# Recurrence of a two-part network: inverse blocks across the array's halves, step products on four quarters, narrower masked copies, both half products ahead of the steps

## The reference, cut to what matters

```python
def rwkv7_scan(r, w, k, v, kk, a):
    def step(state, inp):
        r_t, w_t, k_t, v_t, kk_t, a_t = inp
        sa = jnp.einsum('bhvk,bhk->bhv', state, -kk_t)
        state = (state * w_t[:, :, None, :] + sa[..., None] * (kk_t * a_t)[:, :, None, :]
                 + v_t[..., None] * k_t[:, :, None, :])
        return state, jnp.einsum('bhvk,bhk->bhv', state, r_t)
    ...
    _, out = lax.scan(step, jnp.zeros((nB, H, N, N), F32), xs)
```

## Time and profile before

| | |
|---|---|
| runs | 2591.47, 2591.73, 2594.94 us; median 2591.73 |
| profiled execution | span 2590.2 us; no time outside the span is listed for it |
| PE busy | 2488.4 us, 96% |
| DVE busy | 1104.5 us, 43% |
| ACT busy | 475.8 us, 18% |
| POOL busy | 179.1 us, 7% |
| the 80 copies at L3948 | the first at 2068.1, the last at 2337.4 us |
| a middle pair, from one first half product to the next | 35.4 us |

### The profile page before, as it was taken

The page is one execution under the profiler, slowest core; times in us unless marked ns, Lnnn a source line. Parts: engine busy times, 40 slices in busy tenths (PEclk is TensorE's granted clock), DMA queues, the critical chain, the costliest instruction groups (busy, mean ns, idle before and its releaser), DMA issues. The chain is left out here.

```text
span 2590.2 us, 80261 instructions
## 1 busy us (share of the span) xinstructions
PE 2488.4 (96%) x36137; PEld 2147.1 (83%) x36137; DVE 1104.5 (43%) x2659; ACT 475.8 (18%) x1059; POOL 179.1 (7%) x225
## 2 busy tenths in 40 slices
PE   8999999999999999999999999899999999999998
PEld 7898878789889989999989898677768677877775
DVE  4672554468211010110110102457672578775676
ACT  2112000211123223210000001410010444542000
POOL 0100000010022322210000000000000001110000
PEclk9999999999989999999999999999999999999999
DMA  7444444554589999999999998335653000020443
GB/s 228 156 147 149 162 162 149 162 163 147 208 317 407 407 407 408 407 408 407 407 407 408 407 407 277 122 98 194 220 172 130 3 7 7 7 70 25 163 172 120
DMA packets 289906, 571.50 MB, mean 221 GB/s; under 512 B 17422, under 2 KB 180244, under 8 KB 289764
## 3 DMA queue, kind: packets, MB, share of 16 engines
q1 hardware_dynamic: 289764, 569.49, 60.0%
HBM read 568.37 MB, written 5.28 MB: 221 GB/s over the span
## 5 line engine op out<-in xcount | busy, mean ns | idle before, releaser
L2669 PE MATMUL ps<-xg,ring 128*64 128x80 f32 x14336 | 508.4, 233 | 6.4 <-issue 4.8
L2669 PEld LDWEIGHTS ps<-xg,ring 128*64 128x64 f32 x14336 | 501.8, 137 | 11.0 <-issue 6.6
L2792 DVE TENSOR_TENSOR hidden<-acted,ps 128x320 f32<-128x320 f32 x64 | 28.6, 446 | 662.2 <-PE ps L2669 662.2
L2685 PE MATMUL ps<-hidden,expert_down 128*64 128x80 f32 x7168 | 258.4, 234 | 11.0 <-DMA expert_down<-in_moe_w_down_dram 5.2
L2685 PEld LDWEIGHTS ps<-hidden,expert_down 128*64 128x64 f32 x7168 | 252.8, 138 | 13.9 <-issue 9.7
L2734 ACT ACTIVATE ring<-second 128x1792 f32<-128x1792 f32 x60 | 101.9, 1699 | 212.7 <-PE ps L2669 156.3
L631 PE MATMUL ps<-xT,ring 128*128 128x256 f32 (+1 forms) x592 | 134.4, 387 | 3.0 <-PEq L474 3.0
L631 PEld LDWEIGHTS ps<-xT,ring 128*128 128x128 f32 (+1 forms) x592 | 108.0, 185 | 26.7 <-issue 3.5
L2726 POOL COPY ring<-second 128x1792 f32<-128x1792 f32 x60 | 101.0, 1683 | 311.1 <-PE ps L2669 183.8
L631 PE MATMUL ps<-ring,xT 128*128 128x256 f32 (+1 forms) x544 | 108.9, 361 | 2.2 <-PEq L1136 2.2
L631 PEld LDWEIGHTS ps<-ring,xT 128*128 128x128 f32 x544 | 96.0, 190 | 14.5 <-issue 3.0
(11 more groups left out here) (617 smaller groups left out, 3980.4 us busy)
## 6 DMA issues: line engine op xcount, KB each, us to landing
expert_down<-in_moe_w_down_dram SPq DMA_DIRECT2D x96, 1024.0 KB, 17.1
ring<-in_mlp_w_dram SPq DMA_DIRECT2D x64, 1024.0 KB, 5.3
ring<-in_moe_w_gate_dram SPq DMA_DIRECT2D x68, 896.0 KB, 16.0
ring<-in_moe_w_up_dram SPq DMA_DIRECT2D x68, 896.0 KB, 16.6
second<-in_moe_w_gate_dram SPq DMA_DIRECT2D x30, 1792.0 KB, 18.8
second<-in_moe_w_up_dram SPq DMA_DIRECT2D x30, 1792.0 KB, 19.0
ring<-in_w_xkv_dram SPq DMA_DIRECT2D x16, 1024.0 KB, 5.4
expert_down<-in_moe_w_down_dram SPq DMA_DIRECT2D x32, 512.0 KB, 16.5
```

What stands on the lines that cost most here:

```text
L2669: mm = pe.matmul(bank[b][o:o + HEAD, at, :], w[:, c, f * P + o:f * P + o + HEAD], xg[:, p * E_STEP + c, :], start=(p == 0 and c == 0 and a ...
L2685: mm = pe.matmul(yT[c // 4][o:o + HEAD, c % 4, :], w[:, j, c * P + o:c * P + o + HEAD], hidden[:, f, :], start=False, stop=False, skip_gro ...
L2792: dve.tensor_tensor(hidden[:, part, :], acted[:, part, :], src, ALU.mult).then_inc(hidden_ready, 1)
```

## The change

- The mask `level` is cut to 64 columns: for each level the columns of the upper kind that can change, then those of the lower kind. `XX` and `M1` are flat arrays of 9 x 64 now, in two regions of 4 x 64 (kind 0 and kind 1, swapped for d = 1). `moved` picks, out of both regions, the half of the columns that a level can change: runs of 2^k columns, with as many left out between them. The copies in `front` and `step` move these alone: 256 elements per partition in place of 512, at the last level 128 in place of 256.
- The transposed kind lies on the other half of the partitions. `halves` takes its operands from half h and writes to the other half; `steps` has one kind's results on half b and the other kind's on the other half, and one kind in bank A(d), the other in bank B(d) (`made`). So its products go over all four quarters in turn.
- `m1` writes what `XX` now expects; `right_sides`, `take_right`, `solve_first`, `carry`, `take_carried` and `solve_second` change halves accordingly, and the first solve's result goes to bank B(1) (`FIRST`).
- In each level `halves` of both directions come first, at level 1 each with its `rows`; then for each direction the level's other products and `steps`. In the last pair `turn(6)` comes behind the carries.
- The order of DVE, ACT, POOL and SP stays.

```diff
-        level.append(np.tile(np.concatenate([lower, lower.T, lower], axis=1), (2, 1)))
+        low_columns = lower[:, (e[0] // b) % 2 == 0]
+        high_columns = lower.T[:, (e[0] // b) % 2 == 1]
+        level.append(np.tile(np.concatenate([low_columns, high_columns], axis=1), (2, 1)))
...
-        M1 = [tmp(ctx, "M1", [P, 4, 2, HEAD]) for _ in range(2)]
-        XXs = [[tmp(ctx, "XX", [P, 4, 2, HEAD]) for _ in range(2)] for _ in range(2)]
+        M1 = [tmp(ctx, "M1", [P, 9 * HEAD]) for _ in range(2)]
+        XXs = [[tmp(ctx, "XX", [P, 9 * HEAD]) for _ in range(2)] for _ in range(2)]
...
+        def region(kind, d):
+            return kind if d == 0 else 1 - kind
+
+        def XX(i, d, kind, n):
+            at = (4 * region(kind, d) + n) * HEAD
+            return XXs[d][i % 2][:, at:at + HEAD]
+
+        def whole(i, d):
+            return XXs[d][i % 2][:, 0:8 * HEAD]
+
+        def moved(flat, k):
+
+            b = 1 << k
+            regions = flat[:, 0:2 * (4 * HEAD + b)].rearrange("p (r x) -> p r x", r=2)[:, :, 0:4 * HEAD]
+            return regions.rearrange("p r (n m z b) -> p r n m z b", n=4, z=2, b=b)[:, :, :, :, 0, :]
+
+        def places_of(k):
+            b = 1 << k
+            return level[:, k, :].rearrange("p (r m b) -> p r m b", r=2, b=b).unsqueeze(2).to_broadcast([P, 2, 4, HEAD // 2 // b, b])
...
+        FIRST = B(1)
+
+        def both_kinds(d):
+
+            return ps[:, A(d):B(d) + 1, :].rearrange("p a b -> p (a b)")[:, 4 * HEAD:]
+
+        def made(d, kind, n):
+
+            at = n * HEAD
+            if region(kind, d):
+                return ps[:, B(d), at:at + HEAD]
+            return ps[:, A(d), 4 * HEAD + at:4 * HEAD + at + HEAD]
...
                 def halves(i, k, d):
                     wait(pe, "x_ready", i, 2 * (k - 1) + d + 1)
                     for n in range(4):
                         for b in range(2):
-                            h = half(b)
-                            mm = pe.matmul(ps[h, A(d), n * HEAD:(n + 1) * HEAD], GM[d][h, n, 0, h], XX(i, d)[h, n, 0, :], start=True, stop=True)
+                            h, other = half(b), half(1 - b)
+                            mm = pe.matmul(ps[other, A(d), n * HEAD:(n + 1) * HEAD], GM[d][h, n, 0, h], XX(i, d, 0, n)[h], start=True, stop=True)
                     mm.then_inc(q["half_done"].sem, 1)
...
-                                h = half(b)
-                                xt, p = XX(i, d)[h, n, 1, :], Pb[d][h, n, :]
-                                at = (2 * n + kind) * HEAD
-                                mm = pe.matmul(ps[h, B(d), at:at + HEAD], p if kind else xt, xt if kind else p, start=True, stop=True)
+                                other = half(1 - b)
+                                xt, p = XX(i, d, 1, n)[other], Pb[d][other, n, :]
+                                on = other if kind else half(b)
+                                mm = pe.matmul(made(d, kind, n)[on], p if kind else xt, xt if kind else p, start=True, stop=True)
...
                             halves(i, k, d)
                             if k == 1:
                                 rows(i, d)
+                        for d in range(2):
+                            if k == 1:
                                 rest(i, 0, d)
...
                     outputs(i, 0, 1)
+                    for d in range(2):
+                        carry(i, 1, d)
                     if last:
                         turn(6)
-                    for d in range(2):
-                        carry(i, 1, d)
...
-                    places = level[:, 0, d * HEAD:(d + 2) * HEAD].unsqueeze(1).to_broadcast([P, 4, 2 * HEAD])
-                    dve.copy_predicated(XX(j, d)[:].rearrange("p n k e -> p n (k e)"), places, M1[d][:].rearrange("p n k e -> p n (k e)"))
+                    dve.copy_predicated(moved(XXs[d][j % 2][:], 0), places_of(0), moved(M1[d][:], 0))
...
-                    x = XX(i, d)[:].rearrange("p n k e -> p n (k e)")
-                    made = ps[:, B(d), :].rearrange("p (n e) -> p n e", n=4)
-                    a, e = (HEAD if k == LEVELS - 1 else 0), 2 * HEAD
-                    places = level[:, k, d * HEAD + a:d * HEAD + e].unsqueeze(1).to_broadcast([P, 4, e - a])
-                    dve.copy_predicated(x[:, :, a:e], places, made[:, :, a:e]).then_inc(q["x_ready"].sem, 1)
+                    x, fresh, places = moved(XXs[d][i % 2][:], k), moved(both_kinds(d), k), places_of(k)
+                    if k == LEVELS - 1:
+                        x, fresh, places = (z[:, region(1, d)] for z in (x, fresh, places))
+                    dve.copy_predicated(x, places, fresh).then_inc(q["x_ready"].sem, 1)
```

More of the change, by code:

```diff
@@ L3078, in __init__ @@
         self.keep = tmp(ctx, "keep", [P, 2, 3 * P])
-        self.level = tmp(ctx, "level", [P, LEVELS, 3 * HEAD], I32)
+        self.level = tmp(ctx, "level", [P, LEVELS, HEAD], I32)
         self.eyes = tmp(ctx, "eyes", [P, HEAD])
@@ L3449, in begin @@
                     for d in range(2):
-                        act.activation(XX(j, d)[:].rearrange("p n k e -> p (n k) e"), eyes[:].unsqueeze(1).to_broadcast([P, 8, HEAD]), ACT.Copy).then_inc(q["x_begun"].sem, 1)
+                        act.activation(whole(j, d).rearrange("p (n e) -> p n e", e=HEAD), eyes[:].unsqueeze(1).to_broadcast([P, 8, HEAD]), ACT.Copy).then_inc(q["x_begun"].sem, 1)
                 def exps_first(j, d):
@@ L3581, in m1 @@
                         for kind in range(2):
-                            for hh, b in CORNERS:
+                            at = (2 * region(kind, d) + t) * HEAD
+                            for hh, on in CORNERS:
+                                b = 1 - on if kind else on
                                 a, e = KR(j, d)[half(hh), t, 0, half(b)], Bs[d][half(hh), t, half(b)]
-                                at = (2 * t + kind) * HEAD
-                                mm = pe.matmul(ps[half(b), A(d) + hh, at:at + HEAD], e if kind else a, a if kind else e, start=True, stop=True)
+                                mm = pe.matmul(ps[half(on), A(d) + hh, at:at + HEAD], e if kind else a, a if kind else e, start=True, stop=True)
                     mm.then_inc(q["m1_done"].sem, 1)
@@ L3642, in right_sides @@
                         left = GM[d][:, 2 * t + hh, 2, :]
[L3643 to L3644 removed]
+                        pe.matmul(ps[g, G(d), at:at + HEAD], left[:, f], values(i, t, hh), start=(hh == 0), stop=(s == 0 and hh == 1))
+                        mm = pe.matmul(ps[f, G(d), at:at + HEAD], left[:, g], values(i, t, hh), start=(hh == 0), stop=False)
                     if s:
                         s0 = S0[d][:].rearrange("p a b -> p (a b)")
[L3647 to L3648 removed]
+                        pe.matmul(ps[g, G(d), RIGHT:RIGHT + P], KR(i, d)[:, t, 0, f], s0, start=False, stop=True)
+                        mm = pe.matmul(ps[f, G(d), RIGHT:RIGHT + P], KR(i, d)[:, t, 0, g], s0, start=False, stop=False)
                     mm.then_inc(q["right_done"].sem, 1)
@@ L3675, in solve_first @@
                     wait(pe, "right_ready", i, 2 * s + d + 1)
-                    f = half(d)
+                    f, g = half(d), half(1 - d)
                     for hh in range(2):
                         at = SOLVED + hh * HEAD
-                        mm = pe.matmul(ps[f, G(d), at:at + HEAD], XX(i, d)[f, 2 * chunk(s, d) + hh, 1, :], rhs[d][f, s, hh, :], start=True, stop=True)
+                        mm = pe.matmul(ps[f, FIRST, at:at + HEAD], XX(i, d, 1, 2 * chunk(s, d) + hh)[g], rhs[d][g, s, hh, :], start=True, stop=True)
                     mm.then_inc(q["first_done"].sem, 1)
@@ L3686, in carry @@
                         at = RIGHT + hh * HEAD
-                        mm = pe.matmul(ps[g, G(d), at:at + HEAD], GM[d][f, 2 * t + hh, 0, g], sa[d][f, t, hh, :], start=False, stop=(hh == 1))
+                        mm = pe.matmul(ps[f, G(d), at:at + HEAD], GM[d][f, 2 * t + hh, 0, g], sa[d][f, t, hh, :], start=False, stop=(hh == 1))
                     mm.then_inc(q["carried_done"].sem, 1)
@@ L3691, in solve_second @@
                     wait(pe, "carried_ready", i, 2 * s + d + 1)
-                    g = half(1 - d)
+                    f, g = half(d), half(1 - d)
                     for hh in range(2):
                         at = SOLVED + hh * HEAD
-                        mm = pe.matmul(ps[g, G(d), at:at + HEAD], XX(i, d)[g, 2 * chunk(s, d) + hh, 1, :], rhs[d][g, s, hh, :], start=True, stop=True)
+                        mm = pe.matmul(ps[g, G(d), at:at + HEAD], XX(i, d, 1, 2 * chunk(s, d) + hh)[f], rhs[d][f, s, hh, :], start=True, stop=True)
                     mm.then_inc(q["second_done"].sem, 1)
```

10 lines of the change are left out of this document (4 added, 6 removed).

## The result

The changed kernel takes **2603.57 us** (median of six runs, 2597.07 to 2612.8), the kernel before 2592.15 on the same chips (six runs, 2591.47 to 2594.94). The ratio is 1.0046, 95% interval 1.0029 to 1.0063: **slower by about half a per cent**, and more scattered. The forecast was 2589.7 and "no change"; the time lies inside the range of 2575 to 2605, the sign was given 0.26.

What follows compares the result with a forecast made beforehand. It took the bound to be the chain between PE's products and DVE's in-order queue, not either engine's busy time. Six middle pairs +1.2, first -0.5, last -2.7: -2.0 us, 2588.2 profiled, 2589.7 median; range 2575 to 2605.

Steps and rivals of the forecast that it cites:

- no change: The worked forecast for the whole kernel: within 0.2% (5.2 us) of the kernel before; chance 0.43 in all.
- the sign: Whole kernel slower than before: chance 0.26, against 0.31 for faster and 0.43 for within 0.2%.
- S in four quarters: Step's product at levels 1 to 4 goes from 0.93 to 0.47 us: 29.8 us less work for PE.
- Rival C: In the step's product, row halves sharing a bank take turns, so it stays 0.93: slower, 2605 us; chance 0.06.
- The order eats the gain: Direction 1's half product, put forward, waits for DVE's copy; middle pair 0.2 us longer despite 3.7 less PE work.
- Rival B: DVE's pieces don't hold up direction 1's half products; the full 29.8 us come out: 2562, half 2577; chance 0.20.
- The short copies: Masked copies of 256 elements last 0.44 us and hold DVE's queue 0.34, in place of 0.72 and 0.62.
- its other case: Front copies: if single words cost what the length saved, level 1, direction 1's half product comes 0.23 us later; 1.8 total.
- Rival D: Masked copies keep 0.62 us of queue because runs are short: 2.3 per pair, about 17 in all, 2607; chance 0.08.
- The last pair: Recurrence's last pair, without factor pieces on DVE: last result at 20.98, 2.7 us shorter than before.
- The first pair: Recurrence's first pair, without output pieces on DVE: result at 23.14, 0.5 us shorter than before.
- rival E: PE's idle spots in each pair halve the clock for a tenth of the recurrence: 10 to 15 us, 2603; chance 0.06.

Runs made afterwards that it cites:

- order_hold: Kernel before with both half products first in each level, plus 2, 1 and 2 unread products at levels 2, 3 and 5: 2620.09 us, ratio 1.0109.
- quarters_full: Changed kernel with PE's order of before and masked copies of all columns, leaving only the four quarters: 2574.65 us, ratio 0.9939.
- hold_full: Changed kernel with 3, 2 and 3 unread products at levels 2, 3 and 5 and masked copies of all columns: 2611.15 us, ratio 1.0079.
- old_order: Changed kernel with PE's order of before in the levels, four quarters and narrow copies kept: 2567.3 us, ratio 0.9911.
- hold2: Changed kernel with 2, 1 and 2 unread products filling PE's gaps at levels 2, 3 and 5: 2592.39 us, ratio 1.0007.
- order_only: Kernel before with only the new order of PE, both half products first in each level: 2630.5 us, ratio 1.0157.
- hold: Changed kernel with 3, 2 and 3 unread products filling PE's gaps at levels 2, 3 and 5: 2596.12 us, ratio 1.002.
- dve_early: Changed kernel with DVE's factor and output pieces moved behind the copies of levels 1 and 2: 2593.98 us, ratio 1.001.

## Why the prediction was right and wrong

Middle pair, each at a granted clock of 1.00, from the runs above:

| | new order off | new order on |
|---|---|---|
| two quarters, full copies | 35.40 (before) | 39.58 (order_hold) |
| four quarters, full copies | 33.2 (quarters_full) | 38.25 (hold_full) |
| four quarters, narrow copies | 32.10 (old_order) | 36.25 (hold2) |

The changed kernel is the lower right cell with the clock falling: 37.7 to 40.7. The right column contains the unread products, which order_only's second pair shows to add nothing in the upper cell; hold_full has the larger set of them (hold's, whose pair is 0.15 over hold2's). Views of the cells that no line above shows (quarters_full, order_hold, hold_full):

```profile
2161.70:2194.90 33.20, 29.80 (x765) 24.74 (x760) 27.70 (x79) 17.96 (x55) 3.25 (x8) 1.00 0.03 7
2179.40:2219.00 39.60, 36.47 (x784) 30.21 (x777) 28.00 (x79) 18.13 (x55) 3.24 (x8) 1.00 0.02 6
2177.00:2215.25 38.25, 34.57 (x780) 27.82 (x776) 27.90 (x79) 17.83 (x55) 3.25 (x8) 1.00 0.02 6
```

**S in four quarters: right.** 0.47 per S. Rival C (a bank shared by row halves) falls: the Trainium skill's Gotcha 1 in "TensorEngine Tiling (Array Packing)", that different row tiles cannot access one PSUM bank at the same time, isn't borne out by this trace, in which the 32 records of an S start within 0.47 us, 16 into each of two banks, and each bank is written from both row halves, in different partitions.

**The order eats the gain: right in mechanism and place.** Rival B (0.20) falls with 31.0 us of waiting for DVE. The order alone costs 4.2 per pair in the first and the last row of the table (39.58 - 35.40; 36.25 - 32.10), and about 4.9 in the middle one (38.25 - 33.2, less the 0.15 of the larger set): the parts don't simply add up, since with the new order the full copies cost more. The chain, counted from the pair's first H, against hold2:

| | forecast | hold2 |
|---|---|---|
| copy[1,0] | 4.72 | 4.90 |
| copy[1,1] | 6.73 | 7.10 |
| H[2,1] | 7.22 | 7.87 |
| copy[2,0] | 9.51 | 10.21 |
| copy[3,0] | 14.65 | 15.37 |
| copy[4,1] | 20.22 | 20.9 |
| last copy | 23.64 | 24.2 |
| pair | 35.6 | 36.25 |

**The short copies: a term mis-sized.** The 0.65 arises before H[2,1], and the rest of the chain only carries it. Front and level 1 copies were put at 0.34 of queue and 0.44 of duration. They took 0.52 and 0.51 of queue (0.18 each, so H[1,1] came at 1.16 in place of 0.98, near the 0.23 that the prediction had as its other case, and copy[1,1] by 0.19 more), and the level 1 copy's result came 0.77 after its start (2185.97 to H at 2186.74) in place of 0.49. Rival D was right in the main for runs of one and two columns (0.52 and 0.51 of queue, where it had 0.62), and wrong for four and more (0.33). Its limit was misworked: by its own 17 us for 0.28, the 0.2% band is left from some 0.46 of queue on, not 0.42. With this, six middle pairs cost 5.1 and not 1.2. The last pair of hold2 gives 2.7, as forecast (its last copy 25.28 after its first front copy, before 27.97). The first pair is 0.55 longer, where I had 0.5 shorter; the 0.65 explains part of that, the rest I haven't traced. Sum +3 in place of -2, and the runs of hold2 say +1: with the clock held, the kernel is where the forecast put it, within 0.2% of before.

**The clock: the step that failed.** This is what moved the time out of "no change": with the clock held, hold2 is at a ratio of 1.0007. I had seen the idle spots (1.5, 1.2, 0.5 and 1.6 per pair; measured, in the pair shown, 1.52 at level 2, 0.27 at 4 and 1.40 at 5, and 0.94 at level 3 in the pairs in which the clock is full again by then), named rival E with its price, 10 to 15 us and 2603, and gave it 0.06, on the ground that the pair before has idle spots too. That argument was too weak: it set spots of 0.3 to 0.5 against three of over a microsecond, and asked no row what follows such a one. Before has one, 1.59 behind the recurrence, and its clock stayed at 1.00, so that row wouldn't have settled it either:

```profile
2382.38 0.89 PE L2045 MATMUL ps<-xT,ring 128*128 128x256 f32 x3 [1.59 <-PEq L3419]
```

order_only shows the fall without quarters and narrow copies, old_order shows none in the recurrence with both, and hold2 removes it by filling the gaps: the cause is the idle that the order makes, and its price here is some 10 us of the median. In the profiled execution it was more, 19.3 us over seven pairs (272.4 from the first pair's front copy to the last pair's, against 253.1 in hold2). This also goes with the scatter: the six runs go from 2597.07 at a mean granted clock of 0.991 to 2612.8 at 0.981. What decides in which pairs the clock falls stays open.

That 2603.57 lies inside the range is luck: its upper end, 2605, came from rival C, which fell, and not from the clock.

What was to prove the forecast wrong did so: a middle pair over 36.2.

## What to carry to other kernels

Moving a waiting instruction forward on an engine that runs in order saved its wait here only at the price of longer ones, since the engine that releases it had no slack there; read that engine's queue between the two releases before moving, and move its work with it. When an edit turns covered time on TensorE into idle time, price the clock as well: here some 10 us, more than anything left over from the edit itself. And of a change in several parts, time each alone: two parts worth some 23 us (old_order against before) were hidden under a third that cost some 35 (ratio 1.0046 against 0.9911).

## What the runs showed of the hardware that I had not expected

- In pairs in which PE idled for 1.52 us at level 2 and 1.34 to 1.40 at level 5, the granted clock fell from 1.00 to 0.50 (2.4 to 1.2 GHz) around these places; with unread products in the same gaps it stayed at 1.00, and the kernel with more work was 10 us faster. How much of a pair ran so varied: of the first seven pairs in the profiled execution, four had 3.4 us at half clock and three 13.6; the eighth had none. Spots of that size don't always bring it: order_only's second pair kept 1.00 with waits of 1.40, 1.03 and 1.63, and dve_early's with one of 1.83.
- A masked copy of 256 elements per partition lasts 0.43 if they come in runs of 4 or more (0.39 to 0.45 over all of them; before, in four runs of 64, it took 0.44), 0.71 in runs of 2 (from PSUM) and 0.73 in runs of 1 (from SBUF), against 0.725 for 512 in one piece. The rule in the Trainium skill, "Vector Engine (DVE) Microarchitecture Reference", section 5.2 (full rate from runs of two adjacent words on), agrees for single words, but not for the runs of two of level 1; those are read from PSUM, and no run here has runs of two on SBUF alone. The engine's queue tells the same: 0.52, 0.51 and 0.33 in place of 0.62.
- Sixteen products on four quarters of the array took 0.47, though each of their two banks was written from both row halves.
